# Rotary embedding: the swap of halves by SBUF-to-SBUF transfers from ScalarE's queue in place of products with a sign matrix

## The reference

```
def apply_rope(t, cos, sin):
    t1, t2 = jnp.split(t.astype(jnp.float32), 2, axis=-1)
    c = cos[None, :, None, :]
    s = sin[None, :, None, :]
    return jnp.concatenate([t1 * c - t2 * s, t1 * s + t2 * c], axis=-1).astype(t.dtype)
```

## Time and profile before

| | |
|---|---|
| time, median of 3 runs | 981.78 us (980.66 to 982.83) |
| span of the profiled execution | 979.1 us |
| median less that span | 2.7 us |
| TensorE busy | 946.8 us, 97% |
| VectorE busy | 779.1 us, 80% |
| ScalarE busy | 592.2 us, 60% |
| GpSimd busy | 336.6 us, 34% |
| DMA | 156.27 MB, mean 160 GB/s |

### The profile page before, as it was taken

The page is one execution under the profiler, slowest core; times in us unless marked ns, Lnnn a source line. Parts: engine busy times, 40 slices in busy tenths (PEclk is TensorE's granted clock), DMA queues, the critical chain, the costliest instruction groups (busy, mean ns, idle before and its releaser), DMA issues. The chain is left out here.

```text
span 979.1 us, 15924 instructions
## 1 busy us (share of the span) xinstructions
PE 946.8 (97%) x5735; PEld 781.4 (80%) x5735; DVE 779.1 (80%) x1261; ACT 592.2 (60%) x953; POOL 336.6 (34%) x263
## 2 busy tenths in 40 slices
PE   8999998999999999999999999899999999999997
PEld 6898766777877888888889986677777788888885
DVE  6988999995666887788865689999857678787876
ACT  6446764758454765666664465756764556666654
POOL 0011756671320483156501047668506001111010
PEclk9999999999999999999999999999999999999999
DMA  8953432345544755565468434243735436555551
GB/s 228 261 178 129 130 122 94 124 94 171 171 165 140 198 190 196 175 211 172 134 181 256 151 103 130 86 130 104 196 132 171 130 129 216 195 191 180 195 183 43
DMA packets 135720, 156.27 MB, mean 160 GB/s; under 512 B 16385, under 2 KB 103017, under 8 KB 135658
## 3 DMA queue, kind: packets, MB, share of 16 engines
q1 hardware_dynamic: 135656, 155.46, 51.0%
q10 hardware_dynamic: 2, 0.00, 0.0%
HBM read 154.40 MB, written 1.05 MB: 159 GB/s over the span
## 5 line engine op out<-in xcount | busy, mean ns | idle before, releaser
L1599 DVE TENSOR_TENSOR wl<-ring,wh 128x1024 fp32r<-128x1024 f32 (+1 forms) x276 | 369.2, 1340 | 75.0 <-ACT wh L1288 73.5
L1288 ACT ACTIVATE wh<-ring 128x1024 fp32r<-128x1024 f32 (+1 forms) x276 | 288.8, 1049 | 137.3 <-PE pj L748 107.0
L748 PE MATMUL pj<-h,wh 128*128 128x512 f32 (+1 forms) x1344 | 295.3, 342 | 5.4 <-DVE wl L1599 3.5
L748 PE MATMUL pj<-wh,h 128*128 128x512 f32 (+1 forms) x832 | 274.8, 396 | 9.1 <-ACT gate L1275 5.9
L748 PEld LDWEIGHTS pj<-h,wh 128*128 128x128 f32 x1344 | 227.4, 190 | 33.6 <-issue 5.0
L748 PEld LDWEIGHTS pj<-wh,h 128*128 128x128 f32 x832 | 155.3, 188 | 55.0 <-issue 16.4
L748 PE MATMUL pj<-h,wl 128*128 128x256 f32 x1024 | 188.6, 282 | 0.0
L748 PEld LDWEIGHTS pj<-h,wl 128*128 128x128 f32 x1024 | 157.2, 191 | 6.9
L748 PE MATMUL pj<-wl,h 128*128 128x512 f32 (+1 forms) x416 | 160.0, 385 | 0.0
L2228 POOL TENSOR_TENSOR work<-work 128x512 f32<-128x512 f32 x20 | 41.3, 2063 | 286.6 <-DVE work L2049 191.3
L748 PEld LDWEIGHTS pj<-wl,h 128*128 128x128 f32 x416 | 78.6, 189 | 12.8
(11 more groups left out here) (314 smaller groups left out, 1443.8 us busy)
## 6 DMA issues: line engine op xcount, KB each, us to landing
ring<-in_ffn_w_up SPq DMA_DIRECT2D x44, 1024.0 KB, 5.1
ring<-in_w_in SPq DMA_DIRECT2D x40, 1024.0 KB, 5.1
ring<-in_ffn_w_down SPq DMA_DIRECT2D x22, 1024.0 KB, 4.9
ring<-in_w_in SPq DMA_DIRECT2D x16, 512.0 KB, 5.4
ring<-in_w_branch SPq DMA_DIRECT2D x8, 1024.0 KB, 5.1
ring<-in_w_out SPq DMA_DIRECT2D x8, 1024.0 KB, 5.1
ring<-in_w_branch SPq DMA_DIRECT2D x8, 512.0 KB, 6.1
ring<-in_w_in SPq DMA_DIRECT2D x8, 256.0 KB, 3.4
```

The lines of the kernel that those rows point to most:

```text
L748: return nc.tensor.matmul(o, a, b, start=start, stop=stop, skip_group_check=True)
L1288: A(dst, src, ACT.Copy).then_inc(w_hi.sem, 1)
L1599: TT(dst, src, hi.bitcast(F32), ALU.subtract).then_inc(w_lo.sem, 1)
```

## The change

The sign matrix goes from the constants, and the four TensorE products a layer with it. After `split_hi(2n+4)` of units 2 to 5 ScalarE now issues four transfers within SBUF: each block of 32 partitions of the new tile goes to the block on the other side of its head (`r ^ 32`), into `work[:, 1:3]`. GpSimd and VectorE wait for all four (`rot_in`, 64) in place of the product. The signs are now in the sine table. VectorE multiplies the swapped tile by the sine in place, from SBUF where it was PSUM, and has no wait for the earlier rotary result, as each unit has its own columns.

```
-K_ID, K_ROT, K_TRI, K_NEG1 = 0, 128, 256, 384
...
+K_ID, K_TRI, K_NEG1 = 0, 128, 256
...
+    k[:, K_SIN:K_SIN + T] = np.tile(np.concatenate([-sn, sn]), (2, 1))
...
+        swapped = work[:, 1:3].rearrange("p n c t -> p (n c t)")
...
+        rot_in = [sem(f"rot_in{i}", 64) for i in range(4)]
...
+        def rope_at(n):
+            return (0, 2 * T, 3 * T, 5 * T)[n - U_K], (2, 1, 2, 2)[n - U_K]
...
-                rotate(bO, kr[:, 0:2, :], U_K)
-                rotate(bX[1], kr[:, 2:3, :], U_K + 1)
                 narrow(U_U)
-                rotate(bA, qr[:, 0:2, :], U_Q)
-                rotate(bB, qr[:, 2:4, :], U_Q + 1)
                 narrow(U_U + 1)
...
+            def swap_halves(l, n, src):
+                a.wait_ge(unit_out[n % 2].sem, unit_out[n % 2].at(l, n // 2 + 1))
+                first, m = rope_at(n)
+                for r in range(0, P, 32):
+                    to = r ^ 32
+                    a.dma_start(swapped[to:to + 32, first:first + T * m].rearrange("p (m t) -> p m t", m=m),
+                                src[r:r + 32, 0:m, :]).then_inc(rot_in[n - U_K].sem, rot_in[n - U_K].up(16))
...
                     split_hi(l, 2 * n + 4)
+                    if n < U_U:
+                        swap_halves(l, n, dst)
...
+                    v.wait_ge(rot_in[n].sem, rot_in[n].at(l, 64))
+                    first, m = rope_at(U_K + n)
+                    r2 = swapped[:, first:first + T * m].rearrange("p (m t) -> p m t", m=m)
+                    TT(r2, r2, sin_b.broadcast_to([P, m, T]), ALU.mult).then_inc(dve_step.sem, dve_step.up())
...
-                    g.wait_ge(rot_done.sem, rot_done.at(l, n + 1))
+                    g.wait_ge(rot_in[n].sem, rot_in[n].at(l, 64))
```

More of the change, by code:

```diff
@@ L149 @@
 SPLIT_AT = {q: S_FILL + 2 + q for q in range(1, 37)} | {(32 if j < 7 else 36) + 2 * j: S_Y + j for j in range(3, 10)}
-K_ID, K_ROT, K_TRI, K_NEG1 = 0, 128, 256, 384
[L153 to L160, removed]
+K_ID, K_TRI, K_NEG1 = 0, 128, 256
+K_COS, K_SIN = 384, 640
+K_MASK = 896
+K_CMASK = 1152
+K_PAR = 1184
+K_NPAR = 1186
+K_HALF = 1188
+K_SUM = 1190
+K_ALL = 1222
 A_D, A_PK, A_PV, A_PKS = 16, 64, 80, 112
@@ L175, in constants @@
     k[:, K_ID:K_ID + P] = np.eye(P)
[L177 to L182, removed]
     k[:, K_TRI:K_TRI + P] = -(i[:, None] >= i[None, :]).astype(np.float32)
@@ L323, in build @@
         cP = cE[:, :, 0:NC]
-        rt = work[:, 0, 0, :]
+        swapped = work[:, 1:3].rearrange("p n c t -> p (n c t)")
         blk = s5a[:, :, :].rearrange("p a b -> p (a b)").rearrange("p (r g n a) -> p r g n a", r=2, g=2, a=L2)
@@ L419, in build @@
         dve_step = sem("dve_step")
-        rot_done = sem("rot_done", 4)
+        rot_in = [sem(f"rot_in{i}", 64) for i in range(4)]
         rot_cos = sem("rot_cos", 4)
@@ L865, in narrow @@
                         piece(l, 2 * n + m, pj[n % 2][:, T * m:T * m + T]).then_inc(w_used.sem, w_used.up())
[L867 to L871, removed]
                 for n in range(U_K, U_U):
@@ L1801, in _ @@
                 sin_b = kon[:, K_SIN:K_SIN + T].rearrange("p (o t) -> p o t", o=1)
[L1802 to L1810, removed]
+                for n, dst in enumerate((kr[:, 0:2, :], kr[:, 2:3, :], qr[:, 0:2, :], qr[:, 2:4, :])):
+                    v.wait_ge(rot_in[n].sem, rot_in[n].at(l, 64))
+                    if l == 0 and n == 0:
+                        v.wait_ge(consts_in.sem, 16)
+                    first, m = rope_at(U_K + n)
+                    r2 = swapped[:, first:first + T * m].rearrange("p (m t) -> p m t", m=m)
+                    TT(r2, r2, sin_b.broadcast_to([P, m, T]), ALU.mult).then_inc(dve_step.sem, dve_step.up())
                     v.wait_ge(dve_step.sem, dve_step.last())
@@ L2160, in _ @@
                 for n, dst in enumerate((kr[:, 0:2, :], kr[:, 2:3, :], qr[:, 0:2, :], qr[:, 2:4, :])):
-                    g.wait_ge(rot_done.sem, rot_done.at(l, n + 1))
+                    g.wait_ge(rot_in[n].sem, rot_in[n].at(l, 64))
+                    if l == 0 and n == 0:
+                        g.wait_ge(consts_in.sem, 16)
                     TT(dst, dst, cos_b.broadcast_to([P, dst.shape[1], T]), ALU.mult)\
```

1 line of the change is left out of this document (removed).

## The result

The changed kernel takes 984.16 us (median of 20 runs) against 981.08 (20 runs): a ratio of 1.0023, 95% interval 1.0015 to 1.0032. The ratio compares the means (983.5 and 981.1) and gives 2.3 us slower, where 2.3 us faster was forecast; the medians lie 3.1 us apart. 984.16 is just outside the stated range of 976.0 to 984.0.

A forecast was written before the change was run, and what follows sets the result against it. TensorE, 97% busy, was taken to bound the kernel, with layer 0 held by three resources. Layer 1's 2.7 us won less layer 0's 0.4 lost gave 2.3 off: 979.5 us, range 976.0 to 984.0.

The forecast's parts named there:

- the landing of the transfers: Swap transfers within SBUF land in 2.3 us; three of four units have many microseconds before VectorE wants them.
- the weights in layer 1: ScalarE in layer 1's rotation: it waits for no weights there, so swap traffic was charged no delay.
- The whole amount to be won: TensorE's sign-matrix products, removed: 2.99 us a layer, 5.98 us in all.
- The issues: ScalarE's 32 added DMA issues, four a unit: 0.52 us each, 2.1 us a unit, costing nothing.
- The rule built on it: ScalarE's idle time before the next split covers four issues up to 1.13 us each; beyond, 0.1 us costs 0.4 a unit.
- the one small load: The profile row of a 32 KB DMA that took 2.3 us, taken as nearest to a swap transfer.
- The 1 MB row of 9.4 us: A 1 MB DMA's landing in the busy stretch, held against by another queue and small transfers.
- The rival that had this: The fourth unit lands late behind weights: layer 1 loses 1.1 us, layer 0 about 2.5, 985.4 us; chance 0.10.
- the 2.1 us of delay: Layer 0's second awaited weights, behind 0.66 MB of swap traffic: 2.1 us later at most.
- GpSimd on VectorE: GpSimd's products hold up VectorE through shared SBUF ports: 0.7 to 1.25 us for each meeting a busy VectorE.
- The layers: Compression ends 2.7 us earlier in layer 1 and 0.4 us later in layer 0: 2.3 us off.
- a sign of being right: TensorE waits on VectorE in layer 0, near 45 to 48 us growing from 0.91 towards 2.9, and before the compression.

The follow-up runs named there:

- e3: The changed kernel without any transfers, the swapped columns holding zeros so the output lacks the sine part; 978.71 us, ratio 0.9965 to the kernel before.
- e4: The changed kernel with transfers of 16 columns for 256, same number of issues, a sixteenth of the bytes; 978.10 us, ratio 0.9959 to the kernel before.
- e8: The changed kernel with ScalarE's four transfers a unit replaced by four ScalarE copies, full computation without DMA; 977.45 us, ratio 0.9959 to the kernel before.
- e6: The changed kernel with the fourth unit's transfers alone, the other three units reading zeros; 979.63 us, ratio 0.9981 to the kernel before.
- e7: The changed kernel with the first three units' transfers alone, the fourth unit reading zeros; 978.69 us, ratio 0.9980 to the kernel before.
- e5: The changed kernel with 5 and 3 idle TensorE products ahead of the two compression sets; 982.33 us, ratio 1.0009 to the kernel before.
- e12: The changed kernel with idle products, 5 and 3 ahead of the compression sets and 8 in the gate wait; 979.74 us, ratio 0.9986 to the kernel before.
- e10: The kernel before with 8 idle products a layer in TensorE's merge gate wait; 979.18 us, ratio 0.9976 to the kernel before.
- e9: The changed kernel with ScalarE copies for transfers, plus 8 idle products a layer in the gate wait; 975.42 us, ratio 0.9944 to the kernel before.

## Why the prediction was wrong

In short: two steps failed, the landing of the transfers, put at 2.3 us and no cost, and the weights in layer 1, put at no delay. A third term, the clock behind TensorE's waits, was not in the sum at all. The whole amount to be won was right.

**The amount to be won.** Right. 5.98 us of products went, and e3 shows that 3.4 us of them reach the end by the ratio, 4.1 to 4.6 by the fit, with all of layer 1's among them. In the changed kernel's layer 1 they still reach the compression: TensorE was done with what stands before it 32.0 us after the stage's start, where it had been 34.9. But the compression ended only 0.6 us earlier (36.7 for 37.3), where I had 2.7; 0.7 us of the gap is the second set at half clock (1.77 us for 1.11).

**The issues.** 0.52 us was low: four took 2.4 to 3.5 us, 0.61 to 0.87 each. The rule built on it held by itself, that up to 1.13 us each they hide behind ScalarE's idle time (e4, e8). In the changed kernel part of that idle time was gone, spent on late weights, and the splits stood behind the issues; what that cost was not measured apart.

**The landing.** This step failed. I took 2.3 us from the one small load and left the rest to a rival with a chance of 0.10. The transfers took 4.9 to 5.7 us in the median, and the fourth unit's were in 5.1 us after the last issue. The small row was wrong as a guide even for small transfers: 4 KB took 4.8 us in the same place, at no cost to the time (e4). What a late landing costs is what it releases: GpSimd's last product then ran beside the fourth rotary, and VectorE's addition waited 1.27 us for it (in e6 the multiplication took 1.80 for 0.69). In place of "no cost" it is 1.6 us by the ratio and 1.2 by the fit (e6). The 1 MB row of 9.4 us was no bound to set aside: both were in the same busy stretch. The rival that had this, 985.4 us, lies near the result by luck in part: it asked for a landing of 7 us or more and had no clock in it. The Trainium skill ("DMA: Bandwidth & Descriptors", "Issuing engines are not separate DMA queues") says that DMAs of different engines end up on the same DMA engines and interleave. The trace agrees: 64 KB took 5.6 us on a queue of its own, while the DMA engines' busy share was 1.03 from 25 to 60 us and 1.09 and 1.10 from 530 to 538.

**The weights in layer 1.** This failed too, by an omission. "In layer 1 it waits for no weights there" was read from the kernel before, and the 2.1 us of delay that the same paragraph works out was used for layer 0 alone. With it ScalarE waits 0.88 and 1.15 us in layer 1. In layer 0 the second weight was 3.2 us later against the stage's start (25.4 for 22.3), not 2.1 at most. The first three units cost 1.5 us by the ratio and 2.6 by the fit (e7). In the changed kernel's layer 1 the third rotary ended at 541.1, 1.1 us later than I had worked out from the stage's start (537.0, shifted by 3.0), and the fourth at 544.9, 2.2 later: half of the delay was there before the fourth unit's landing added the rest.

**GpSimd on VectorE.** Right in kind and size: a piece of 1.23 us took 2.22 beside GpSimd's first product at 35.5 us, the last multiplication 1.78 for 0.69. It comes on top of late landings and late weights (e7), since these decide when GpSimd's products run.

**The layers.** With the clock kept, layer 0 loses 1.2 us (I said 0.4, bound 2.0) and layer 1 wins 1.3 (I said 2.7, bounds 2.1 and 3.2). The sum is 0.1 us faster in the profiles, and 0.6 (medians) to 1.0 us (ratios) slower in the timed runs, where I had 2.3 faster.

**The clock.** No step of the prediction had it. The waits ahead of the compression, which I had listed as a sign of being right, are followed by half clock in both layers, 3.4 us at a time. Filled with idle products they are not, and 1.4 us come back (e5). So of the 4.6 us between forecast and result by the ratios, 1.4 are the clock. The rest, 3.2, no kernel measured as a sum; it is what late weights, late landings and GpSimd's products behind them leave. By e12 against e10 the clock's part is 1.3 (ratios) to 1.7 us (medians), and by the fit 1.4 to 2.0, as the change is then only 0.3 to 0.8 us slower than the kernel before. The gate wait's falls cost both kernels alike (0.24% before, 0.23% between e5 and e12) and explain none of the difference of the timed runs. The single profiles differ by 4.8 us, of which 1.6 is a gate fall that the one of before happened to have in one layer only. Nor does each wait bring a fall: the changed kernel waits 1.73 us at 56.31 and stays at 1.00. The Trainium skill ("TensorE: Matmul & The Clock Gate", "What's actually happening") says that the reduced rate is the default and activity lifts it. With the second half the runs agree: 8 idle products in a wait of 2.5 us kept the clock at 1.00 (e9, e10, e12).

Not settled: what of e7's cost is the late weight, what the issues behind it, and what GpSimd's products, which come late for the same reason; and whether all transfers together cost more than the two parts. No kernel separated them.

## What to carry to other kernels

A transfer that was to replace a small product was paid for in its bytes, and mostly by others: with the DMA engines busy all the time the loads behind it came later. So add its traffic to each load in each stage, also where nobody waits yet. Do not take its landing from a quiet place: here the medians were 4 to 6 us at any size from 2 to 64 KB. Ask what the landing releases and whom that holds up. An engine with idle time in the same place (here ScalarE, copying 32 partitions across) did the same for nothing. And a gain that ends in a short wait of TensorE can lose more than the wait: look at the granted clock behind each wait, and try idle products no longer than it. Last, compare executions at the same mean clock before you price a small step.

## What the runs showed of the hardware

- TensorE's clock fell to half for 3.4 us behind some stretches with waits of 0.9 to 2.5 us and not behind others (2.52 us at 635 us of the kernel before). Each fall in the gate wait cost 1.6 us of span here; ten profiles with one and four without agree within 0.3 us.
- Transfers within SBUF from ScalarE's queue landed in 4.9 to 5.7 us for 32 and 64 KB, and in 4.2 to 5.4 us for 2 and 4 KB (medians), in stretches where the DMA engines were busy.
- An idle product of 128 columns in float32 is two instructions of 0.12 us; ten take 2.4 us.
- ScalarE copies 32 partitions of 512 columns to 32 other partitions in 0.65 us (four in 2.60), against 0.60 for a copy of 128 partitions from PSUM to the same partitions.
- Four DMA issues by ScalarE took 2.4 to 3.75 us. SyncE was issuing at the same time in both cases (2.44 us at 53.77 in the changed kernel, 3.75 at 527.24 in e7), so that does not tell them apart.
- The kernel before gains 0.24% by 8 idle products a layer in a wait.
